# Four light experts side by side in the third and fourth expert stages of a diffusion trunk

## The chip, the cores and the metric

The kernel runs on one core of a Trainium2 chip. The metric is the device time of one execution, in microseconds (us). The engines are TensorE (PE, matrix products), VectorE (DVE), ScalarE (ACT), GpSimd (POOL) and SyncE (SP, whose queue issues the transfers from HBM); SBUF is the on-chip memory of 128 partitions, PSUM the eight banks of 128 x 512 float32 that TensorE writes.

## The reference

One inference step of a trunk of four layers over 256 tokens (128 context, 128 latent) of 1024 channels. Each layer has a token mixer (in turn Hyena convolution, gated linear attention, FNet transform, pooling) and then a mixture of experts, each with normalization and a conditioned shift and scale. The change touches the experts:

```python
def hier_moe(h, w_rg, w_re, w1, w3, w2):
    ...
    p_grp, g_idx = lax.top_k(pg, 1)                       # one of 4 groups
    ...
    pe_top, e_idx = lax.top_k(jax.nn.softmax(le, axis=-1), 2)   # two of its 4 experts
    ...
    hid = jax.nn.silu(jnp.einsum('nd,xdf->nxf', xt, w1)) * jnp.einsum('nd,xdf->nxf', xt, w3)
    y = jnp.einsum('nxf,xfd->nd', hid * combine[..., None].astype(hid.dtype), w2)
```

There are 16 experts, each with w1 and w3 of 1024 x 512 and w2 of 512 x 1024, all float32. A token uses two of the 16, so an expert sees 32 of the 256 tokens on average.

## The kernel before

**The expert stage.** Every expert is computed for 64 slots (`SLOTS`): a selection matrix `sel`, built by VectorE from the tokens' ranks within an expert (`build_sel`), gathers tokens into slots by matmul (`gather`), and a transposed one scatters the results back (`scatter`). If an expert has more than 64 tokens, a further round of all experts runs (`rounds_known`, `far_rounds`); with these inputs none is needed. Experts p and p + 8 form pair p, eight pairs per stage, p0 to p7 (`PAIRS`), computed side by side in TensorE: the stationary operand is the 128 x 64 block of gathered tokens of one expert, the moving one 512 columns of its weights, and the two experts of a pair write the two halves of the partitions of one bank, in different column groups of the array. A pair takes 8 steps of the contraction for w1 (`experts_in`, kind 0), 8 for w3 (kind 1), and 4 for each of the two halves of w2's output (`experts_out`, kind 2). Between w1, w3 and w2 TensorE does the previous pair's scatter, a part of the next couple's gather and two kinds of transposes. Two pairs form a couple (`COUPLES`), which share one `sel`.

**The weights' way in.** One list, `piece_stream()`, fixes the order in which all weights are loaded by SyncE's queue: conditioning maps (`ada`), mixer weights, experts. They go through a ring of 14 slots (`RING`) of 8 KB per partition, that is 1.049 MB or one slab each. A matrix of a pair is four slabs (`SLABS`, q = 0 to 3); slab q holds the contraction's rows 2q and 2q + 1 (of eight blocks), for both experts. For pairs after the first, two slabs go in one transfer of 2 MB (`in_halves`, `second_half`). Before each transfer SyncE waits until the slot's last content has been used, by counters that TensorE raises (`freed`, `h1_mm`, `h3_mm`, `y_mm`); its queue is strictly in order, so what stands behind a waiting transfer waits with it. Four more slabs have a home in another part of SBUF (`homes`): first the w2 of p0, loaded ahead during the mixer (`first_w2`), and after that the w1 of p2 (`homed`), as soon as p0's w2 has been used. Ahead of a stage are thus loaded: w2, w1 and w3 of p0, w1 of p1 and half of its w3.

**Routing.** After the router's matmul VectorE works out, in a chain of small instructions that each wait for the one before (`chain`), each token's group, its two experts, their shares (`comb`) and its rank in each (`rank`), then the number of rounds. In the first three stages a conditioning map is computed beside it (`beside`, `ada_rows`, `ada_mod`).

Of the kernel before, what the change touches and what calls it, by code (L numbers as in the profile page):

```python
# [19 lines left out]
G = 2  # L20
# [12 lines left out]
PAIRS = EXPERTS // 2  # L33
RING = 14
# [86 lines left out]
def piece_stream():  # L121
# [26 lines left out]
    for i in range(LAYERS):  # L148
        experts = [("moe", i, p, kind, q) for p in range(PAIRS) for kind in range(3) for q in range(SLABS)
                   if p or kind < 2]  # L150
# [20 lines left out]
def homed(what):  # L171

    return what[0] == "moe" and what[2:4] == (2, 0)


def in_halves(what):

    return what[0] == "moe" and what[2] > 0 and what[2:4] != (PAIRS - 1, 2)


def second_half(what):
    return in_halves(what) and what[4] % 2 == 1


def build(nc, a):
# [21 lines left out]
    with ctx:  # L207
# [22 lines left out]
        over = sb("over", [1, 2], I32)  # L230
        bank = [ctx.enter_context(nc.psum_tensor(f"bank{i}", [P, 512], F32)) for i in range(8)]
# [59 lines left out]
        selw = ar(7168, 2, G, 2, SLOTS)  # L291
        rt = ar(7424, 240)
        comb = ar(7680, G, EXPERTS)
        memb = ar(7712, EXPERTS).bitcast(BF16).rearrange("p (g n) -> p g n", g=G)
        rank = ar(7744, G, EXPERTS)
        wcol = ar(7816, 1)
# [4 lines left out]

        def home_pair(i, h):
            return ar(homes[i][h], 2 * SLAB)
# [53 lines left out]
        def freed(what):  # L357
# [14 lines left out]
            if k == "moe":  # L372
                return USED[what[3]], primed(SLABS * (PAIRS * what[1] + what[2]) + what[4] + 1)
# [17 lines left out]
        def expert_slab(n, q):  # L391
            return a["moe_w"][bass.ds(n, 1)][:, :, SLAB * (q % 2):SLAB * (q % 2) + SLAB].rearrange("o p n -> p (o n)")

# [41 lines left out]
        def _(sp):  # L437
# [4 lines left out]
            last = {}  # L442
            for what, slot, nth in stream:
# [8 lines left out]
                if what[0] == "first":  # L452
# [8 lines left out]
                    for q in range(SLABS):  # L461
                        sp.dma_start(first_w2[i][q], expert_slab(6 * PAIRS * i + 4 + q // 2, q)) \
                            .then_inc(s("first_w2_loaded"), 16)
# [4 lines left out]
                if what[0] == "moe" and what[1] < LAYERS - 1 and what[2:] == (1, 1, 2):  # L468
# [10 lines left out]
                    sp.dma_start(rw[:], a["router"][i + 1]).then_inc(s("rw_loaded"), 16)  # L479
                if homed(what):  # L480
                    _, i, p, kind, q = what
                    if q % 2:
                        sp.wait_ge(s("y_mm"), primed(SLABS * PAIRS * i + q + 1))
                        sp.dma_start(home_pair(i, q // 2), a["moe_w"][6 * (PAIRS * i + p) + 2 * kind + q // 2]) \
                            .then_inc(s(f"homed{q // 2}"), 16)
                    continue
# [3 lines left out]
                last[slot] = freed(what)  # L490
                if in_halves(what):
                    _, i, p, kind, q = what
                    if q % 2:
                        sp.dma_start(ring_all[:, SLAB * (slot - 1):SLAB * (slot + 1)],
                                     a["moe_w"][6 * (PAIRS * i + p) + 2 * kind + q // 2]) \
                            .then_inc(s(f"full{slot - 1}"), 16)
                    continue
                if what[0] == "moe":
                    _, i, p, kind, q = what
                    src = expert_slab(6 * (PAIRS * i + p) + 2 * kind + q // 2, q)  # L500
                else:
                    src = source(what)
                sp.dma_start(ring[slot], src).then_inc(s(f"full{slot}"), 16)

            def one_round(b, i):
                for kind in range(3):
                    sp.wait_ge(s(USED[kind]), primed(SLABS * PAIRS * (i + 1)))
                with sp.Fori(0, COUPLES) as c:
                    for j in range(2):
                        for kind in range(3):  # L510
                            sp.wait_ge(s("fb_" + USED[kind]), primed(SLABS * (2 * (b + c) + j)))
                            for q in range(SLABS):
                                sp.dma_start(ring[where["moe", i, 1, kind, q][0]][:],
                                             expert_slab(6 * (PAIRS * i + j) + 2 * kind + q // 2 + 12 * c, q)) \
                                    .then_inc(s(f"fb_full{kind}"), 16)
                for kind in range(3):
                    sp.wait_ge(s("fb_" + USED[kind]), primed(SLABS * 2 * (b + COUPLES)))
# [143 lines left out]
        def _(pe):  # L661
# [102 lines left out]
            def experts_in(pre, n, kind, x, j, weights, ready):  # L764

                for q in range(SLABS):
                    w = weights(kind, q).rearrange("p k (e n) -> p k e n", e=2)
                    ready(q)
                    for kk in range(2):
                        k = 2 * q + kk  # L770
                        for e in range(2):
                            at = P * e + SLOTS * j
                            last = mm(bank[4 + kind][SLOTS * e:SLOTS * e + SLOTS, :], x[:, k, at:at + SLOTS],  # L773
                                      w[:, kk, e, :], start=k == 0, stop=k == KD - 1)
# [8 lines left out]
            def slot_weights(pre, n, j):  # L783
                for g in range(G):
                    last = tr(bank[5][:, g * P:g * P + P], selw[:, j, g].rearrange("p e n -> p (e n)"), ident)
                last.then_inc(s(pre + "selT_mm"), 1)

            def experts_out(pre, n, weights, ready):
                pe.wait_ge(s(pre + "hidT_ready"), primed(n + 1))
                for q in range(SLABS):  # L790
                    w = weights(2, q).rearrange("p f (e n) -> p f e n", e=2)
                    if q % 2 == 0:
                        ready(q // 2)
                    for ff in range(2):
                        f = 2 * (q % 2) + ff
                        for e in range(2):
                            last = mm(bank[6 + q // 2][SLOTS * e:SLOTS * e + SLOTS, :],  # L797
# [1222 lines left out]
```

## Time and profile before

| | |
|---|---|
| median of 3 runs | 1402.37 us (1401.28 to 1403.22) |
| profiled execution, its own time | 1400.19 us |
| its span, first to last instruction | 1398.0 us |
| TensorE busy | 1343.8 us, 96% |
| VectorE busy | 473.5 us, 34% |
| moved by DMA | 554.37 MB, mean 397 GB/s |
| mean granted clock of TensorE | 0.995 |

Busy time is the time in which at least one instruction of an engine runs. The float32 matmuls appear as two records each, and records of different column groups overlap, so that the busy time of a group of rows divided by its count, not the mean of one record, is what one record costs. The chain of work that ended last goes back from the last instruction to whatever released it, step by step. The granted clock is given as a share of TensorE's full clock.

### The profile page before, as it was taken

To read this page: it belongs to the slowest core of one execution; us is meant where nothing else is said; L and a number is where in the kernel's file an instruction comes from. 1 tells how busy PE (TensorE), PEld (TensorE's weight loads), DVE (VectorE), ACT (ScalarE), POOL (GpSimd) and SP (SyncE) were. 2 spreads that over 40 slices of the span, in tenths; PEclk is the share of its full clock that TensorE was granted. 3 is DMA by queue.
4 is the path that set the end of the run, shared out by engine and by line. 5 is a ranking of instruction groups with operands and counts; after the bars stand their busy time and mean duration, and the time that the engine had idled before them with its cause. 6 is when DMAs were issued, how large, how long until landed. Compare 5 with 4: busy or idle time off the path is not lost.

```text
span 1398.0 us, 17305 instructions
## 1 busy us (share of the span) xinstructions
PE 1343.8 (96%) x7140; PEld 743.5 (53%) x7140; DVE 473.5 (34%) x1067; ACT 286.2 (20%) x514; POOL 32.1 (2%) x30
## 2 busy tenths in 40 slices
PE   9999999999988899999999988999999999999996
PEld 4786585444434688775444424854444356444433
DVE  3787514111114797624112113141111144111113
ACT  3311024111103122224111103241111035111102
POOL 0001310000000000010000000100000000000000
PEclk9999999999999999999999999999999999999999
DMA  9997999999999995789999999889999998999995
GB/s 384 420 398 271 421 420 414 428 427 427 428 428 418 422 406 227 264 357 407 428 426 428 428 428 419 349 364 414 427 428 428 427 419 359 407 426 428 427 427 210
DMA packets 55654, 554.37 MB, mean 397 GB/s; under 512 B 6097, under 2 KB 8081, under 8 KB 9233
## 3 DMA queue, kind: packets, MB, share of 16 engines
q1 hardware_dynamic: 53792, 551.19, 94.7%
q10 hardware_dynamic: 1778, 2.01, 0.4%
q8 instruction: 59, 0.97, 0.3%
q14 instruction: 25, 0.20, 0.0%
HBM read 551.08 MB, written 2.10 MB: 396 GB/s over the span
## 4 chain that ended last, share of the span: by engine, by line
PE 79%; DMA 16%; DVE 2%; ACT 1%; SPq 1%; issue 0%; POOL 0%; DVEq 0%; POOLq 0%
PE bank L773 26%; PE bank L719 14%; PE bank L797 13%; DMA ring<-in_moe_w 10%; PE bank L738 5%; DMA ring<-in_w_ada 4%; PE bank L756 4%; PE bank L679 3%; PE bank L565 2%; DMA ring<-in_hy_w_in 2%; PE bank L693 2%; PE bank L549 1%; PE bank L1022 1%; PE bank L906 1%; PE bank L629 1%; PE bank L623 1%
## 5 line engine op out<-in xcount | busy, mean ns | idle before, releaser
L773 PE MATMUL bank<-ring,hT 128*64 128x512 f32 x1024 | 225.3, 594 | 0.0
L773 PE MATMUL bank<-ring,arena 128*64 128x512 f32 x896 | 199.6, 595 | 22.3 <-DMA ring<-in_moe_w 22.3
L797 PE MATMUL bank<-ring,arena 128*64 128x512 f32 x896 | 198.5, 595 | 0.0
L1533 DVE TENSOR_TENSOR rows<-rows,bank 128x512 f32<-128x512 f32 x32 | 22.0, 688 | 456.5 <-PE bank L773 456.5
L773 PEld LDWEIGHTS bank<-ring,hT 128*64 128x64 f32 x1024 | 72.1, 137 | 139.3 <-issue 137.6
L773 PEld LDWEIGHTS bank<-ring,arena 128*64 128x64 f32 x896 | 63.8, 137 | 150.7 <-issue 128.3
L797 PEld LDWEIGHTS bank<-ring,arena 128*64 128x64 f32 x896 | 61.7, 137 | 116.9 <-issue 115.2
L1552 DVE SCALAR_TENSOR_TENSOR yv_rest<-bank,arena,yv_big 128x512 fp32r<-128x512 f32 x64 | 48.0, 750 | 199.9 <-ACT yv_big L1221 199.9
L719 PE MATMUL bank<-hT,ring 128*128 128x256 f32 x512 | 112.0, 380 | 0.3 <-DMA ring<-in_hy_w_in 0.3
L719 PEld LDWEIGHTS bank<-hT,ring 128*128 128x128 f32 x512 | 96.6, 190 | 15.1 <-issue 2.2
L1221 ACT ACTIVATE yv_big<-bank,arena 128x512 fp32r<-128x512 f32 x64 | 44.0, 688 | 281.0 <-PE bank L797 281.0
L719 PE MATMUL bank<-arena,ring 128*128 128x256 f32 x384 | 83.8, 380 | 1.6 <-DVE arena L1746 0.9
L719 PEld LDWEIGHTS bank<-arena,ring 128*128 128x128 f32 x384 | 72.6, 190 | 12.6 <-DVE arena L1746 1.2
L679 PE MATMUL bank<-ring,condT 128*32 128x512 f32 x576 | 69.1, 598 | 2.5 <-DMA ring<-in_w_ada 1.8
L738 PE MATMUL bank<-sel,htok_big 128*128 128x256 f32 x256 | 68.0, 301 | 0.8 <-DVE sel L1520 0.8
L756 PE MATMUL bank<-selT,yv_big 128*128 128x256 f32 x256 | 66.7, 297 | 1.7 <-DVE yv_rest L1552 1.7
L738 PE MATMUL bank<-sel,htok_rest 128*128 128x256 f32 x256 | 63.2, 282 | 0.0
L756 PEld LDWEIGHTS bank<-selT,yv_big 128*128 128x128 f32 x256 | 48.0, 188 | 28.5 <-issue 26.0
L756 PE MATMUL bank<-selT,yv_rest 128*128 128x256 f32 x256 | 62.2, 279 | 0.0
L1214 ACT ACTIVATE rows<-bank 128x512 f32<-128x512 f32 x32 | 19.1, 598 | 206.2 <-PE bank L773 206.2
L738 PEld LDWEIGHTS bank<-sel,htok_big 128*128 128x128 f32 x256 | 48.3, 189 | 23.7 <-issue 20.5
L1485 DVE CUSTOM_DVE_ANT_0 arena<-ring,vec 128x1024 bf16<-128x1024 f32 x48 | 58.2, 1275 | 6.3 <-DMA ring<-in_w_ada 6.2
(227 smaller groups left out, 1375.8 us busy)
## 6 DMA issues: line engine op xcount, KB each, us to landing
ring<-in_moe_w SPq DMA_DIRECT2D x152, 2048.0 KB, 18.5
ring<-in_w_ada SPq DMA_DIRECT2D x96, 1024.0 KB, 14.8
ring<-in_moe_w SPq DMA_DIRECT2D x48, 1024.0 KB, 23.6
arena<-in_moe_w SPq DMA_DIRECT2D x16, 1024.0 KB, 14.6
arena<-in_moe_w SPq DMA_DIRECT2D x8, 2048.0 KB, 9.7
ring<-in_hy_w_in SPq DMA_DIRECT2D x12, 1024.0 KB, 27.3
ring<-in_hy_w_out SPq DMA_DIRECT2D x4, 1024.0 KB, 14.0
ring<-in_gla_w_v SPq DMA_DIRECT2D x4, 1024.0 KB, 26.2
```

Source lines behind the costliest of these rows:

```text
L565: last = mm(bank[b][:, 256 * (c % 2):256 * (c % 2) + 256], hT[:, k, g], w8[:, k, :], start=k == 0, stop=k == KD - 1)
L679: last = mm(ada_bank(n)[32 * j:32 * j + 32, :], condT[:, G * k:G * k + 32], w[:, j, :], start=k == 0, stop=k == KD - 1)
L693: ins = mm(bank[6][:, 0:NT], ones[:], hT[:, k].rearrange("p g t -> p (g t)"), start=k == 0, stop=k == KD - 1)
L719: last = mm(dst, w[:, k, (m % 2) * P:(m % 2) * P + P], (hT[:, k] if rhs is None else rhs[:, k]).rearrange("p g t -> p (g t)"), start=k == ...
L738: last = mm(bank[b][:, (k % 2) * NT:(k % 2) * NT + NT], htok[n % 2][:, n // 2, k * P:k * P + P], sel[:, n // 2].rearrange("p e j n -> p (e ...
L756: last = mm(half(m), part[:, m * P:m * P + P], selT[:], start=first_pair and m % 2 == 0 and part is yv[0], stop=False, skip_group_check=True)
L773: last = mm(bank[4 + kind][SLOTS * e:SLOTS * e + SLOTS, :], x[:, k, at:at + SLOTS], w[:, kk, e, :], start=k == 0, stop=k == KD - 1)
L797: last = mm(bank[6 + q // 2][SLOTS * e:SLOTS * e + SLOTS, :], hidT[:, f, SLOTS * e:SLOTS * e + SLOTS], w[:, ff, e, :], start=f == 0, stop= ...
L1221: act_fn(yv[0][:, 512 * h:512 * h + 512], bank[6 + h][:], ACT.Identity, scale=wcol) \
L1485: v.tensor_tensor_reduce(junk[at % len(junk)], w, cond_wide[n][:, g], 1.0, b_ada(i, 16 * q + j, 1), ALU.mult, ALU.add, mod[:, i, 16 * q + ...
L1533: tt(sil[:], sil[:], bank[5][:], ALU.mult).then_inc(s(pre + "hid_ready"), 1)
L1552: stt(yv[1][:, cols], bank[6 + h][:], wcol, yv[0][:, cols].bitcast(F32), ALU.mult, ALU.subtract) \
```

## The change

In the third and fourth expert stages (`QUADS`, layers 2 and 3 counted from 0) the eight pairs become six pairs and one unit of four experts with 32 slots each. VectorE sorts the 12 experts outside pairs 0 and 1 by their number of tokens (`order_experts`); the four lightest form the last unit, and SyncE reads the order from SBUF (`value_load`) and loads each pair's weights by it. If one of the four has more than 32 tokens, a further round runs. The weights of these stages are stored expert by expert: a transfer of 2 MB brings both halves of the contraction of one expert's matrix, in the order of slabs 0, 2, 1, 3 (slab 2h + e is half h of expert e). The matrix of p2 with a home is now w2 (kind 2) instead of w1 (kind 0). TensorE's counters rise once per half of a matrix instead of once per slab, in all four stages. In the first three stages the copy `ada_rows` moves ahead of the shares.

```diff
+QUAD = PAIRS - 2
+QUAD_SLOTS = 32
+QUADS = (2, 3)
+UNITS_TO = [sum(QUAD + 1 if i in QUADS else PAIRS for i in range(n)) for n in range(5)]
...
+        if i in QUADS:
+            experts = [("moe", i, p, kind, q) for p in range(QUAD) for kind in range(3)
+                       for q in ((0, 2, 1, 3) if p else range(SLABS)) if p or kind < 2]
+            experts += [("moe", i, p, kind, 2 * h + e) for kind in range(2) for p in (QUAD, QUAD + 1) for e in range(2)
+                        for h in range(2)]
+            experts += [("moe", i, p, 2, 2 * h + e) for h in range(2) for p in (QUAD, QUAD + 1) for e in range(2)]
...
 def homed(what):
-    return what[0] == "moe" and what[2:4] == (2, 0)
+    return what[0] == "moe" and what[2:4] == (2, 2 if what[1] in QUADS else 0)
...
 def second_half(what):
-    return in_halves(what) and what[4] % 2 == 1
+    return in_halves(what) and (what[4] >= 2 if what[1] in QUADS else what[4] % 2 == 1)
...
-                return USED[what[3]], primed(SLABS * (PAIRS * what[1] + what[2]) + what[4] + 1)
+                return USED[what[3]], primed(2 * (UNITS_TO[what[1]] + (min(what[2], QUAD) if what[1] in QUADS else what[2])) + what[4] // 2 + 1)
...
+                if what[0] == "moe" and what[1] in QUADS and what[2] >= FIXED and what[3:] == (0, 0):
+                    i, p = what[1:3]
+                    sp.wait_ge(s("order_known"), QUADS.index(i) + 1)
+                    for e in range(2):
+                        n = (PAIRS - FIXED) * e + p - FIXED
+                        expert[p, e] = sp.value_load(order[0:1, n:n + 1], min_val=EXPERTS * QUADS.index(i),
+                                                      max_val=EXPERTS * QUADS.index(i) + EXPERTS - 1)
...
+            def columns(j, quad=False):
+
+                if quad:
+                    return [(P * e + SLOTS * jj, QUAD_SLOTS) for jj in range(2) for e in range(2)]
+                return [(P * e + SLOTS * j, SLOTS) for e in range(2)]
+
+            def experts_in(pre, i, n, kind, x, cols, weights, ready):
+
+                for h in range(2):
+                    ws = weights(kind, h)
+                    for kk in range(4):
+                        k = 4 * h + kk
+                        if kk % 2 == 0:
+                            ready(k // 2)
+                        for o, (at, m) in enumerate(cols):
+                            last = mm(bank[4 + kind][m * o:m * o + m, :], x[:, k, at:at + m], ws[o][kk] if i not in QUADS else ws[o][:, kk, :],
+                                      start=k == 0, stop=k == KD - 1)
                     last.then_inc(s(pre + USED[kind]), 1)
...
+            def order_experts(i):
+
+                N, each = ORDERED, [P, ORDERED, 2, PAIRS - FIXED]
+                chain(v.tensor_copy(two(o_key12), later(o_key)))
+                chain(tt(o_cmp, o_key12.unsqueeze(1).broadcast_to([P, N, N]), o_key12.unsqueeze(2).broadcast_to([P, N, N]),
+                         ALU.is_ge))
+                chain(v.reduce_sum(o_pos, o_cmp, AX.X))
...
+                ordered(two(o_id), iota[:, 0:EXPERTS])
+                ts(order[0:1, :], o_id[0:1, :], EXPERTS * QUADS.index(i) - 1.0, None, ALU.add).then_inc(s("order_known"), 1)
+                for values, out in ((rank, rank0), (comb, comb0)):
+                    for g in range(G):
+                        ordered(later(out[:, g]), values[:, g])
...
-                build_sel("", 0)
+                build_sel("", 0, rank)
+                if beside is not None:
+                    ada_rows(beside)
                 dve.wait_ge(s("route_exp"), 2 * i + 1)
...
+                if i in QUADS:
+                    order_experts(i)
...
-                if beside is not None:
-                    ada_rows(beside)
                 moe_round(i, beside)
```

## Rows read from the trace of the kernel before

**Rows 1.** The page: busy time, GB/s in 40 slices, chain's shares by engine.

```profile
PE 1343.8 (96%) x7140; PEld 743.5 (53%) x7140; DVE 473.5 (34%) x1067; ACT 286.2 (20%) x514; POOL 32.1 (2%) x30
...
GB/s 384 420 398 271 421 420 414 428 427 427 428 428 418 422 406 227 264 357 407 428 426 428 428 428 419 349 364 414 427 428 428 427 419 359 407 426 428 427 427 210
...
PE 79%; DMA 16%; DVE 2%; ACT 1%; SPq 1%; issue 0%; POOL 0%; DVEq 0%; POOLq 0%
```

**Rows 2.** Windows of the third and fourth expert stages; last columns: clock, DMA share, GB/s.

```profile
952.00:956.00 4.00, 4.00 (x22) 1.37 (x20) 0.75 (x1) 0.69 (x1) 0.00 (x0) 1.00 0.85 283
976.00:1100.00 124.00, 124.00 (x642) 52.97 (x639) 19.92 (x32) 14.65 (x23) 0.00 (x0) 1.00 1.01 427
1198.00:1202.00 4.00, 4.00 (x22) 1.42 (x20) 0.75 (x1) 0.69 (x1) 0.00 (x0) 1.00 0.69 217
1202.00:1340.00 138.00, 138.00 (x716) 59.30 (x714) 22.11 (x36) 17.14 (x27) 0.00 (x0) 1.00 1.01 428
```

**Rows 3.** Chain that ended last: start us, us, what (L773 w1 and w3, L797 w2).

```profile
932.31 13.88 PE bank L773 x64
...
955.97 6.87 PE bank L773 x32
...
964.91 7.02 PE bank L773 x32
...
981.71 6.87 PE bank L773 x32
...
1129.86 7.04 PE bank L797 x32
...
1376.00 7.04 PE bank L797 x32
```

**Rows 4.** Timeline of TensorE, p7's w3 in the third stage; in brackets its idle time before.

```profile
1118.65 3.65 PE L773 MATMUL bank<-ring,arena 128*64 128x512 f32 x16 [1.33 <-DMA ring<-in_moe_w]
1123.46 3.65 PE L773 MATMUL bank<-ring,arena 128*64 128x512 f32 x16 [1.15 <-DMA ring<-in_moe_w]
```

**Rows 5.** The page's costliest groups: busy us, mean ns of one, idle before.

```profile
L773 PE MATMUL bank<-ring,hT 128*64 128x512 f32 x1024 | 225.3, 594 | 0.0
...
L679 PE MATMUL bank<-ring,condT 128*32 128x512 f32 x576 | 69.1, 598 | 2.5 <-DMA ring<-in_w_ada 1.8
```

**Rows 6.** Timeline of SyncE's queue at five issues: start us, us, line.

```profile
942.85 0.33 SPq L494 DMA_DIRECT2D ring<-in_moe_w  x1
...
952.57 0.33 SPq L484 DMA_DIRECT2D arena<-in_moe_w  x1
...
962.92 0.33 SPq L494 DMA_DIRECT2D ring<-in_moe_w  x1
...
1199.08 0.33 SPq L484 DMA_DIRECT2D arena<-in_moe_w  x1
...
1209.43 0.33 SPq L494 DMA_DIRECT2D ring<-in_moe_w  x1
```

**Rows 7.** The page's DMA issues: count, KB each, median us from issue to landing.

```profile
arena<-in_moe_w SPq DMA_DIRECT2D x8, 2048.0 KB, 9.7
```

**Rows 8.** Timeline of VectorE, end of the third stage's routing and first product after.

```profile
928.97 0.19 DVE L1645 TENSOR_TENSOR arena<-arena 128x32 f32<-128x32 f32 x1
929.20 0.53 DVE L1648 TENSOR_SCALAR arena<-arena 128x1 f32<-128x1 f32 x3
...
932.74 0.18 DVE L1468 SCALAR_TENSOR_TENSOR scale<-mod,vec 128x16 f32<-128x16 f32 x1
946.35 0.69 DVE L1533 TENSOR_TENSOR rows<-rows,bank 128x512 f32<-128x512 f32 x1 [13.43 <-PE bank L773]
```

**Rows 9.** Windows about the second mixer's start: us, PE busy, PEld, DVE, ACT, POOL, clock.

```profile
470.00:475.00 5.00, 1.82 (x8) 1.26 (x8) 1.94 (x3) 3.08 (x6) 0.00 (x0) 0.98 1.02 423
475.00:480.00 5.00, 3.78 (x11) 3.24 (x12) 3.72 (x8) 1.75 (x2) 0.00 (x0) 0.50 1.03 426
480.00:485.00 5.00, 5.00 (x21) 4.23 (x21) 4.78 (x9) 0.00 (x0) 0.00 (x0) 0.84 1.00 413
```

More of the change, by code:

```diff
@@ L389, in build, with pair_matrix, expert_matrix, slab @@
         USED = ["h1_mm", "h3_mm", "y_mm"]
-        def expert_slab(n, q):
-            return a["moe_w"][bass.ds(n, 1)][:, :, SLAB * (q % 2):SLAB * (q % 2) + SLAB].rearrange("o p n -> p (o n)")
+        def pair_matrix(i, kind, h, p):
+            n = 6 * (PAIRS * (i - sum(m < i for m in QUADS)) + p) + 2 * kind + h
+            return a["moe_w"][bass.ds(n, 1)]
+        def expert_matrix(kind, n):
+            return a["moe_q"][bass.ds(len(QUADS) * EXPERTS * kind + n, 1)]
+        def slab(i, kind, q, p, expert=None):
+            if i in QUADS:
+                n = EXPERTS * QUADS.index(i) + PAIRS * (q % 2) + p if expert is None else expert
+                m, at = expert_matrix(kind, n), q // 2
+            else:
+                m, at = pair_matrix(i, kind, q // 2, p), q % 2
+            return m[:, :, SLAB * at:SLAB * at + SLAB].rearrange("o p n -> p (o n)")
+        def halves(i, kind, x):
+            if i in QUADS:
+                return [[x(2 * h + e).rearrange("p (k n) -> p k n", k=4) for e in range(2)] for h in range(2)]
+            return [[[x(2 * h + kk // 2).rearrange("p (k e n) -> p k e n", k=2, e=2)[:, kk % 2, e] for kk in range(4)]
+                     for e in range(2)] for h in range(2)]
         def prime(eng, *names):
@@ L441, in _ @@
             sp.dma_start(vec[:], a["vec"]).then_inc(s("vec_loaded"), 16)
-            last = {}
+            last, expert = {}, {}
             for what, slot, nth in stream:
@@ L490, in _ @@
                 last[slot] = freed(what)
+                if what[0] == "moe":
+                    _, i, p, kind, q = what
+                    chosen = expert[p, q % 2] if i in QUADS and p >= FIXED else None
                 if in_halves(what):
[L492 to L495, printed above, removed]
+                    if second_half(what):
+                        if i in QUADS:
+                            n = EXPERTS * QUADS.index(i) + PAIRS * (q % 2) + p if chosen is None else chosen
+                            both = expert_matrix(kind, n)
+                        else:
+                            both = pair_matrix(i, kind, q // 2, p)
+                        sp.dma_start(ring_all[:, SLAB * (slot - 1):SLAB * (slot + 1)], both.rearrange("o p n -> p (o n)")) \
                             .then_inc(s(f"full{slot - 1}"), 16)
@@ L498, in _ @@
                 if what[0] == "moe":
-                    _, i, p, kind, q = what
-                    src = expert_slab(6 * (PAIRS * i + p) + 2 * kind + q // 2, q)
+                    src = slab(i, kind, q, p, chosen)
                 else:
```

198 lines of the change are left out of this document (118 added, 80 removed).

## The prediction

> **What bounds the kernel now.** I read the page first: TensorE is busy 96% of the span and the chain of work that ended last is 79% TensorE and 16% DMA [rows 1]. That invites the thought that each TensorE microsecond removed is a microsecond won. The GB/s line speaks against it: the slices of the expert stages stand at 418 to 428, and 428 looks like a ceiling. So I cut the last two expert stages into windows [rows 2]. From 976 to 1100 us and from 1202 to 1340 us the queue moves 427 and 428 GB/s without a break, and the only idle DMA time inside the two stages is where a stage begins.
>
> The two rates, from rows: a pair of experts takes 25.74 us of TensorE (981.71 less 955.97, [rows 3]), and 12 slabs of 1.049 MB, which at 428 GB/s take 2.45 us each, 29.4 us. TensorE is the faster. It lives off what was loaded ahead (14 ring slabs and 4 home slabs, 44 us of transfer) and has used that up by the last pairs: in pair 7 it stops for 1.33 and 1.15 us before two slabs each, and the starts lie 4.8 us apart [rows 4], which is the transfer time of two slabs. So the stage ends when the last slab lands. The matrix h3 of pair 7 is complete at 1123.46, four slabs are still to come, the last at 1123.46 + 9.8 = 1133.3, and the output matmuls end at 1129.86 + 7.04 = 1136.90, 3.6 us behind it [rows 3, 4]. The fourth expert stage repeats this some 246 us later (1376.00 for 1129.86).
>
> The length of such a stage is thus: when the queue starts again after the prefetch is used up, plus the slabs left at 2.45 us each, plus 3.6 us. TensorE's own work is not in that sum.
>
> **What the change takes away.** A unit of 25.74 us in each of two stages. Four experts of 32 columns need as many steps as two of 64: a pair's step is four matmul records of 220 ns (225.3 us over 1024), 0.88 us; a four-expert step would be eight. The conditioning maps already run four 32-column groups side by side: 69.1 us over 576 records is 120 ns, 0.96 us for eight [rows 5]. The eight units become seven, and the last has 24 steps dearer by at most 0.08 us. TensorE is relieved of 25.7 - 1.9 = 23.8 us per stage, 48 in all. By the sum above this is waiting time moved, not time won: worth 0. The Trainium skill (TensorEngine Tiling (Array Packing), When to Use Tiling) promises up to 4x for at most 32 columns, twice what 64 columns get; the trace agrees to within a tenth. If the stages were bound by TensorE, that would give 1402.4 - 47.6 = 1354.8; DMA windows without a gap exclude it.
>
> The bytes stay the same: each expert's matrices are still loaded once.
>
> **What the change moves: the ring.** Two things change in the stream of the two stages. A 2 MB transfer now brings one expert's whole matrix, first and second half of the contraction, where before it brought half of the contraction for both experts. Both its slots are free only when the *whole* previous matrix pair there has been used. And pair 2's matrix at home is now w2, not w1. I walked the queue for the third stage, with p0, p1 for the pairs, and slots counted from the stage's first slab. Before the walk both kernels are alike: p0's w1 and w3 lie in slots 0 to 7, p1's w1 in 8 to 11, half its w3 in 12 and 13, and the rest of p1 is issued up to 942.85 us into slots 0 to 5 [rows 6].
>
> Before: the next in order are pair 2's w1 slabs, at home, free as soon as p0's w2 is used: issued at 952.57 (and 956). DMA idled a little around it: 952 to 956 has 283 GB/s, which is 4 x (1 - 283/428) = 1.4 us lost [rows 2, 6].
>
> After: p2's w1, first expert, goes to slots 6 and 7, which p0's w3 leaves at 932.31 + 13.88 = 946.2 [rows 3]. That is one transfer, 4.9 us of work for the queue. The next, p2's w1 of the second expert, goes to slots 8 and 9, which now hold the *whole* of p1's first expert's w1, used until 955.97 + 6.87 = 962.8; the trace has an issue at 962.92 that waited for just this event [rows 6]. Everything behind it in SyncE's order waits too, pair 2's w2 as well, though its home is long free. So the queue restarts 962.8 - 952.6 = 10.3 us later and has 4.9 us more to do meanwhile: a loss of 5.4 us, a gap of 1.4 + 5.4 = 6.8 us.
>
> Behind the gap I followed each transfer at 4.9 us against the end of the matrix whose slots it takes. A 2 MB transfer that finds the queue nearly empty lands 9.7 us after its issue [rows 7]; those of 962.9 land at 972.6 and 977.5, and the third is due at 982.4. Its slots come free at 964.91 + 7.02 = 971.9, so that it can land at 981.6: the tightest place, 0.8 us in hand. None later idles the queue, and TensorE, in pairs 2 to 5, waits at most 1.5 us. So the gap is never made up, and the last slab lands 5.4 us late, at 1138.7.
>
> **The four-expert unit.** It needs eight slabs before its first matmul (before: two), its w3 eight more, its w2 four and four. By counting back from 1138.7: w1 complete at 1099.4, w3 at 1119.0, w2's first half at 1128.9. TensorE ends pair 5 near 1087, so it idles some 12 us, works 7.4 (1106.8), idles 12, works 7.4 (1126.4), does scatter and transposes in 2.7 us as now, and has the last half of w2's four steps, 3.6 us, left when the last slab lands: 1142.3 against 1136.9, again +5.4. The ring holds 14 slabs and w1 keeps eight: w3's last transfer waits for w1's end at 1106.8, can land 9.7 later at 1116.5, and is due at 1119.0. A margin of 2.5 us.
>
> **The stage after.** The queue and TensorE both enter the fourth mixer 5.4 us late, so the short stall of the queue at that stage's start stays as it is. In the fourth stage the same walk gives 1209.43 - 1199.08 = 10.35 [rows 6], less 4.9 again: +5.4, on a gap of 4 x (1 - 217/428) = 2.0 us [rows 2].
>
> **What is hidden.** The ordering adds some 24 VectorE instructions per stage. Chained small ones cost 0.2 us each here (928.97 is followed by the next at 929.20), those of 144 elements lie between that and the 0.69 us of 512; I take 0.3, 7 us in all, bounds 5 and 16. They cover themselves: VectorE is through at 932.9 and idle 13.4 us until 946.35 [rows 8]. TensorE asks for the new selection at 946.2; at 16 us it would be late by about 3 us, at 7 not at all. The ids that SyncE waits for are ready after the first seven, near 932, long before 943; two register loads follow. The time between 942.85 and 946.2 covers them, and data are then queued until 953. The earlier copy of the conditioning rows moves 0.7 us within the same slack. In the first two stages counts per half instead of per slab can make the last half wait up to 0.5 us for its second slab: +0.3 taken.
>
> **The sum.** 1398.0 of span becomes 1398.0 + 5.4 + 5.4 + 0.3 = 1409.1; the profiled execution took 1400.19, and the median of the runs, 1402.37, lies 2.2 above that. On the median: **1413.5 us**.
>
> **Rivals.**
>
> *The clock.* Between 470 and 480 us TensorE idled 4.4 us, and the granted clock went to 0.50, the lower level, 1.2 GHz [rows 9]; 12 us of idling twice per stage will do so too. If it stays low through the eight steps of w1, they take 14.7 and end at 1114.1; w3's last transfer lands at 1123.8, 4.8 late, and the stage ends that much later. In this trace the low level lasted 5 us and then 0.16/0.5 x 5 = 1.6 more, which costs 3.3 of work: w1 ends at 1110.1, the transfer is 0.8 late, and I leave that to the range. The Trainium skill (TensorE: Matmul & The Clock Gate, HAM oscillation) describes this very pattern, short compute between DMA waits, as one that loses the clock each time; here it would be 1413.5 + 2 x 5 = 1423. For it: the idles are nearly three times the one seen. Against: the loss seen would be hidden but for 0.8. Chance 0.14.
>
> *No gap.* If the queue has other work after 958, or the transfers left are taken faster, both effects vanish and the time is 1402.7. Speaking for it: only my walk through slots, no row, shows the gap; a slot miscounted by two would close it. Chance 0.13.
>
> *Faster.* One mechanism: the transfer issued at 946.2 fills the gaps that the queue has now (1.4 and 2.0 us), and nothing opens in their place; it decides if pair 2's second transfer is issued before 956. Then 1402.4 - 3.4 = 1399.0. A larger gain needs the queue above 428 GB/s, which no window shows. Chance 0.07.
>
> *The light experts are not light enough.* With over 32 tokens for one of the four, a whole further round runs: at least 96 slabs x 2.45 = 235 us, 1640. Counted from the reference's inputs, the four lightest of the twelve have 17, 19, 29, 31 and 19, 22, 26, 30 tokens against 32 slots: held, but 31 by a single token. Chance 0.03.
>
> **Chances and range.** My forecast has 0.63, its own range 1409 to 1418. A measurement of this kernel tells 0.2%, 2.8 us, from no change. Slower: 0.63 + 0.14 + 0.03 = 0.80; within: 0.13; faster: 0.07. The range 1402 to 1422 takes in the forecast, the case of no gap and the smaller half of the clock's.
>
> **What would show it.** About 7 us of idle DMA some 25 us into the third and fourth expert stages, between a transfer issued at the end of p0's w3 and one at the end of p1's w1; TensorE idling 10 us or more before each matrix of the four-expert unit; a granted clock of 0.5 there; DMA at 427 to 428 between; TensorE busy some 45 us less and the span longer. It is wrong if the four-expert unit begins without a DMA wait, or if the queue never idles behind pair 0.

## The result and the profile after

The changed kernel takes 1418.01 us in the median of 4 runs, the kernel before on the same chips 1401.82: ratio 1.0118, 95% interval 1.0100 to 1.0136, 16.2 us slower, and the interval leaves out 1. The forecast was 1413.5, 11.1 us slower; the sign and most of the size are as forecast. The profiled execution has a span of 1414.8 us, 16.8 more than before.

The page of the changed kernel, first its busy time, GB/s and the chain by engine:

```profile
PE 1310.4 (93%) x7096; PEld 729.3 (52%) x7096; DVE 476.8 (34%) x1099; ACT 282.1 (20%) x508; POOL 32.1 (2%) x30
...
GB/s 384 421 385 271 420 421 417 425 428 427 427 426 420 421 414 207 284 346 427 424 428 426 429 422 389 328 427 343 427 426 428 422 421 339 335 428 428 427 425 178
...
PE 77%; DMA 19%; DVE 2%; ACT 1%; issue 1%; POOL 0%; SPq 0%; DVEq 0%; POOLq 0%
```

TensorE is busy 33.4 us less than in [rows 1] and the kernel is longer. (Some 45 us less were forecast; the low clock in the four-expert unit, seen below, gives back about 12: its long rows add up to 47.6 us, and would be 35.6 at the 7.07 and 3.64 us that they take at full clock.) Two new hollows stand in the GB/s line, 343 and 335, each a slice behind the start of an expert stage. SyncE's queue at the issues behind pair 0 of the third stage:

```profile
946.12 0.35 SPq L542 DMA_DIRECT2D ring<-in_moe_q  x1
...
962.74 0.34 SPq L542 DMA_DIRECT2D ring<-in_moe_q  x1
...
971.85 0.33 SPq L542 DMA_DIRECT2D ring<-in_moe_q  x1
```

These are the three times that the prediction worked out by its walk through the ring, 946.2, 962.8 and 971.9. Where [rows 6] have an issue at 952.57, nothing is issued now for 16.6 us. Windows (us, PE busy, PEld, DVE, ACT, POOL, granted clock, DMA share, GB/s): two about this gap, three in the third stage's four-expert unit, one at the start of the fourth stage, two about the gap's twin there, and one at the last matmuls of that stage:

```profile
952.00:958.00 6.00, 6.00 (x30) 2.01 (x28) 1.50 (x2) 1.38 (x2) 0.00 (x0) 1.00 0.94 401
958.00:966.00 8.00, 8.00 (x46) 3.86 (x44) 0.00 (x0) 0.60 (x1) 0.00 (x0) 1.00 0.35 92
1092.00:1105.00 13.00, 4.97 (x24) 1.38 (x28) 0.00 (x0) 0.00 (x0) 0.00 (x0) 0.50 1.00 427
1112.00:1122.00 10.00, 2.48 (x12) 0.68 (x16) 0.00 (x0) 0.00 (x0) 0.00 (x0) 0.52 1.00 419
1139.00:1143.00 4.00, 3.61 (x20) 1.27 (x24) 0.00 (x0) 0.00 (x0) 0.00 (x0) 0.58 1.00 418
1184.00:1193.00 9.00, 9.00 (x53) 4.71 (x53) 7.09 (x27) 3.55 (x5) 0.00 (x0) 1.00 0.29 80
1205.00:1218.00 13.00, 13.00 (x65) 4.73 (x62) 1.50 (x2) 1.97 (x3) 0.00 (x0) 1.00 0.52 220
1218.00:1222.00 4.00, 4.00 (x26) 2.15 (x26) 0.00 (x0) 0.00 (x0) 0.00 (x0) 1.00 0.93 311
1394.00:1400.00 6.00, 5.92 (x32) 1.52 (x32) 0.00 (x0) 0.00 (x0) 0.00 (x0) 0.58 0.01 3
```

Idle DMA in the gap of the third stage: 6 x (1 - 401/428) + 8 x (1 - 92/428) = 6.7 us (forecast 6.8); in the fourth: 13 x (1 - 220/428) + 4 x (1 - 311/428) = 7.4 us (forecast 7.4). The four-expert unit is in the timeline of TensorE, for the third and the fourth stage:

```profile
1100.03 9.76 PE L825 MATMUL bank<-ring,arena 128*32 128x512 f32 x64 [12.47 <-DMA ring<-in_moe_q]
1119.53 8.55 PE L825 MATMUL bank<-ring,arena 128*32 128x512 f32 x64 [9.73 <-DMA ring<-in_moe_q]
...
1130.72 3.64 PE L849 MATMUL bank<-ring,arena 128*32 128x512 f32 x32
1139.39 5.34 PE L849 MATMUL bank<-ring,arena 128*32 128x512 f32 x32 [5.04 <-DMA ring<-in_moe_q]
...
1354.75 8.70 PE L825 MATMUL bank<-ring,arena 128*32 128x512 f32 x64 [12.49 <-DMA ring<-in_moe_q]
1374.24 9.19 PE L825 MATMUL bank<-ring,arena 128*32 128x512 f32 x64 [10.79 <-DMA ring<-in_moe_q]
1386.11 3.64 PE L849 MATMUL bank<-ring,arena 128*32 128x512 f32 x32
1394.08 6.08 PE L849 MATMUL bank<-ring,arena 128*32 128x512 f32 x32 [4.33 <-DMA ring<-in_moe_q]
```

w1, w3 and the last half of w2 wait for their last slab, as forecast, at 1100.0, 1119.5 and 1139.4 (forecast 1099.4, 1119.0, 1138.7); the first half of w2, at 1130.72, does not wait. New is the length of the last row of either stage: the same 32 records take 3.64 us at 1130.72 and 5.34 and 6.08 us at the end, where the windows show a mean granted clock of 0.58. The third stage ends at 1144.8, the fourth at 1400.2, where [rows 3] give 1136.9 and 1383.0: 7.9 and 17.2 us late.

VectorE's part is where it was put: it is through with routing, ordering and selection at 937.9, and then idles 8.2 us, where [rows 8] had 13.4.

```profile
937.68 0.17 DVE L1528 SCALAR_TENSOR_TENSOR scale<-mod,vec 128x16 f32<-128x16 f32 x1
946.02 0.69 DVE L1603 TENSOR_TENSOR rows<-rows,bank 128x512 f32<-128x512 f32 x1 [8.16 <-PE bank L825]
```

### The profile page after: what moved, and what is told of

Its sections match the earlier page's. It is cut to its first block, busy times and chain, and to the rows that moved or that the text cites. A ratio compares the mean times of both kernels' runs of the same rounds, so it can differ in the third digit from the quotient of the medians.

```text
span 1414.8 us, 17531 instructions
## 1 busy us (share of the span) xinstructions
PE 1310.4 (93%) x7096; PEld 729.3 (52%) x7096; DVE 476.8 (34%) x1099; ACT 282.1 (20%) x508; POOL 32.1 (2%) x30
## 4 chain that ended last, share of the span: by engine, by line
PE 77%; DMA 19%; DVE 2%; ACT 1%; issue 1%; POOL 0%; SPq 0%; DVEq 0%; POOLq 0%
PE bank L825 25%; PE bank L765 14%; PE bank L849 11%; DMA ring<-in_moe_q 9%; DMA ring<-in_moe_w 8%; PE bank L784 4%; PE bank L725 3%; PE bank L802 3%; DMA ring<-in_w_ada 2%; PE bank L611 2%; PE bank L739 2%; PE bank L595 1%; PE bank L1082 1%; PE bank L966 1%; PE bank L675 1%; PE bank L669 1%
## 5 line engine op out<-in xcount | busy, mean ns | idle before, releaser
L825 PE MATMUL bank<-ring,arena 128*64 128x512 f32 (+1 forms) x960 | 194.3, 634 | 57.8 <-DMA ring<-in_moe_q 45.5
L849 PE MATMUL bank<-ring,arena 128*64 128x512 f32 (+1 forms) x832 | 175.3, 617 | 10.2 <-DMA ring<-in_moe_q 9.4
L825 PEld LDWEIGHTS bank<-ring,arena 128*64 128x64 f32 (+1 forms) x960 | 61.7, 136 | 183.0 <-issue 168.9
L849 PEld LDWEIGHTS bank<-ring,arena 128*64 128x64 f32 (+1 forms) x832 | 54.8, 136 | 113.5 <-issue 112.0
L1622 DVE SCALAR_TENSOR_TENSOR yv_rest<-bank,arena,yv_big 128x512 fp32r<-128x512 f32 x60 | 45.0, 751 | 202.7 <-ACT yv_big L1281 202.7
L802 PE MATMUL bank<-selT,yv_big 128*128 128x256 f32 x240 | 62.2, 296 | 1.8 <-DVE yv_rest L1622 1.8
L802 PEld LDWEIGHTS bank<-selT,yv_big 128*128 128x128 f32 x240 | 45.0, 188 | 27.1 <-issue 24.4
L802 PE MATMUL bank<-selT,yv_rest 128*128 128x256 f32 x240 | 58.1, 279 | 0.0
## 6 DMA issues: line engine op xcount, KB each, us to landing
ring<-in_w_ada SPq DMA_DIRECT2D x96, 1024.0 KB, 14.7
```

Of the source, the lines that this page charges most:

```text
L802: last = mm(half(m), part[:, m * P:m * P + P], selT[:], start=first_pair and m % 2 == 0 and part is yv[0], stop=False, skip_group_check=True)
L825: last = mm(bank[4 + kind][m * o:m * o + m, :], x[:, k, at:at + m], ws[o][kk] if i not in QUADS else ws[o][:, kk, :], start=k == 0, stop=k ...
L849: last = mm(bank[6 + h][m * o:m * o + m, :], hidT[:, f, m * o:m * o + m], ws[o][f] if i not in QUADS else ws[o][:, f, :], start=f == 0, st ...
L1622: stt(yv[1][:, cols], bank[6 + h][:], wcol, yv[0][:, cols].bitcast(F32), ALU.mult, ALU.subtract) \
```

## The experiments

All ratios are to the kernel before, run on the same chip. Because the profiled executions reach the third stage up to 4.6 us apart, the last columns give each stage by itself in that execution, from its first expert matmul to its last, and the landing of its last slab, read as the start of the matmul that it released; both come from the chain or TensorE's timeline. A dash: TensorE did not wait for that slab, so the time is not seen. "Filling" matmuls (`keep_running`) are products on ones into an unused bank, put where TensorE would idle.

| kernel | ratio (95%) | third stage | fourth stage | last landing, 3rd / 4th |
|---|---|---|---|---|
| before | 1 | 204.6 | 204.2 | - |
| changed | 1.0118 (1.0100 to 1.0136) | 212.8 | 213.5 | 207.4 / 207.4 |
| e1, w1 at home | 1.0071 (1.0050 to 1.0091) | 210.1 | 210.4 | 204.7 / 204.8 |
| e2, clock kept | 1.0103 (1.0076 to 1.0130) | 212.8 | 213.3 | 207.5 / 206.9 |
| e3, both | 1.0072 (1.0052 to 1.0093) | 209.4 | 210.1 | 204.0 / 203.6 |
| e4, no unit | 1.0142 (1.0116 to 1.0168) | 214.0 | 215.5 | - |
| e5, before, TensorE lighter | 0.9976 (0.9968 to 0.9985) | 204.5 | 202.8 | 202.5 / 200.8 |
| e6, single slabs | 1.0086 (1.0073 to 1.0099) | 209.3 | 210.5 | 203.4 / 204.4 |
| e7, e6 and clock | 1.0057 (1.0044 to 1.0070) | 207.9 | 208.3 | 204.2 / 204.6 |
| e8, e7 and end split | 1.0033 (1.0021 to 1.0045) | 207.3 | 206.8 | - / 204.8 |
| e9, clock at the end only | 1.0094 (1.0078 to 1.0109) | 210.8 | 210.9 | 207.2 / 207.2 |
| e10, e9 and end split | 1.0093 (1.0077 to 1.0109) | 210.5 | 210.9 | - |
| e11, mixed | 1.0026 (1.0015 to 1.0036) | 206.8 | 205.1 | - / 203.1 |
| e12, before, single slabs | 1.0026 (1.0017 to 1.0034) | 205.6 | 205.3 | 203.7 / - |

The mixer between the two stages is 41.9 us in every one of them.

**Does TensorE's work count? e5.** In the kernel before:

```diff
-                            last = mm(bank[4 + kind][SLOTS * e:SLOTS * e + SLOTS, :], x[:, k, at:at + SLOTS],
-                                      w[:, kk, e, :], start=k == 0, stop=k == KD - 1)
+                            wide = P if pre == "" and kind == 1 and q > 1 and n >= 2 * PAIRS and n % PAIRS > 1 else 512
+                            last = mm(bank[4 + kind][SLOTS * e:SLOTS * e + SLOTS, 0:wide], x[:, k, at:at + SLOTS],
+                                      w[:, kk, e, 0:wide], start=k == 0, stop=k == KD - 1)
```

> The kernel before, with less work for TensorE in the third and fourth stages and nothing else changed: in pairs 2 to 7 the second half of w3's contraction is computed for 128 of its 512 columns, so a part of the result is left out. It relieves TensorE of 2.6 us per pair, 16 per stage, 32 in all, and loads the same bytes in the same order. Theory (the stages end with the last slab): within 2 us of the kernel before. Rival (TensorE bounds them): 1402 - 32 = 1370.

Measured 1399.12 against 1402.26, 3.1 us less. The 32 us were reckoned too high: by the page TensorE's busy time fell by 23.6 us, from 1343.8 to 1320.2. The last rows of TensorE's w2 in the third and in the fourth stage:

```profile
1135.70 1.94 PE L798 MATMUL bank<-ring,arena 128*64 128x512 f32 x8 [0.55 <-DMA ring<-in_moe_w]
...
1380.37 1.94 PE L798 MATMUL bank<-ring,arena 128*64 128x512 f32 x8 [0.53 <-DMA ring<-in_moe_w]
```

TensorE now waits for the very last slab and does two steps behind it. In the fourth stage that slab lands 200.8 us after the start; in the kernel before TensorE ended at 204.2, 3.4 behind (I had inferred 3.6 from counting slabs). In the third it is 202.5, so that there I had 3.6 where 2.1 is right. This takes e5's landings for those of the kernel before, whose own trace does not show them. Relief thus buys a part of TensorE's lag behind the last landing, not its work: 0.1 and 1.4 us by the two stages of the table, 3.1 by the medians, for 23.6 us less of work. The difference between the two readings was not traced.

**The gap, and the clock. e1, e2, e3.** e1 puts home w1 back, e2 fills the unit's idle time, e3 does both:

```diff
-    return what[0] == "moe" and what[2:4] == (2, 2 if what[1] in QUADS else 0)
+    return what[0] == "moe" and what[2:4] == (2, 0)
```
```diff
+                    if quad:
+                        pe.wait_ge(s("yv_rest"), primed(2 * n))
+                        keep_running(11, wide_ones)
                     experts_in("", i, n, 0, x, cols, weights, gathered_for)
+                    if quad:
+                        keep_running(12, wide_ones)
...
-                    experts_out("", i, n, cols, weights, evacuated)
+                    experts_out("", i, n, cols, weights, (lambda h: keep_running(3 * h, wide_ones)) if quad else evacuated)
```

> The changed kernel with one thing put back: in the third and fourth expert stages the matrix of pair 2 that has a home is w1 again, not w2. Transfers stay one expert's whole matrix each. Theory (the queue's gap behind pair 0): w1's four slabs are issued at about 952 and 956 us, so the gap at 958 to 965 us closes (about 1.4 us of idle DMA left, as before the change), and so does that of the fourth stage; the queue ends each stage 5.4 us earlier than in the changed kernel: 1418.0 - 10.8 = 1407, or a little less. Rival (the four-expert unit with its slow clock costs it all, the gap being made up later): no change, 1416 to 1418.

> The changed kernel with idle-time matmuls on ones into an unused bank in the four-expert unit: 11 before w1, 12 before w3, 3 before the second half of w2, so that TensorE never idles there for long. Theory: the granted clock stays at 1.00, w1 and w3 take 7.2 us instead of 9.8 and 8.6, w2's last half 3.6 instead of 5.3 and 6.1; the stages end 2.5 us (third) and about 6 us less late (fourth, with the start of the stage), so 1418.0 - 6 = 1412, near the sum in which the clock was left out (1413.5). The gap of the queue behind pair 0 stays at 6.7 and 7.4 us. Rival (the clock is a bystander, the transfers land late by themselves): within 2 us of 1418.

> Both of the former in one: pair 2's w1 at home and the idle-time matmuls. Theory: both losses are gone and the saved unit is worth nothing, since the last slab lands when it did before: 1401 to 1403, the time of the kernel before within 0.2%. Rival (TensorE's relief of some 24 us per stage is worth something once nothing else is in its way): under 1398.

e1 won 2.7 and 3.1 us in the two stages, against 5.4 expected in each. The rest is seen in its windows of the third stage:

```profile
952.00:962.00 10.00, 10.00 (x49) 3.30 (x46) 1.50 (x2) 1.38 (x2) 0.00 (x0) 1.00 0.90 331
1000.00:1015.00 15.00, 15.00 (x80) 6.27 (x80) 3.04 (x6) 2.57 (x4) 0.00 (x0) 1.00 0.97 386
```

The big gap has shrunk to 10 x (1 - 331/428) = 2.3 us, but the queue now runs short again at 1000 to 1015, by 1.5 us, which my walk had not looked for: with the queue no longer late, transfers that need a whole matrix's slots find them not yet free. (In the same window e11, whose pairs 1 to 3 go slab by slab, has 422 GB/s, and the kernel before 430.) So the home is about half of the loss and the whole-matrix transfers keep the other half.

e2's ratio, 1.0103, cannot be told from the 1.0118 of the changed kernel, and its stages are 0.0 and 0.2 us shorter, though w1 and w3 now took 7.1 us each. The slow clock in w1 and w3 is harmless to within that, as the prediction's margin had it. The last half of w2 still took 5.34 and 6.40 us: three filling matmuls end 3.5 us before the landing, and behind that pause the clock is low again. e3 therefore keeps that loss too, and came out at 1412, not at 1402. My theory for these three was wrong in its sums, and three terms were open: the end, the whole-matrix transfers, and the steps behind the last landing.

**The clock at the end. e9.**

```diff
                 for h in range(2):
+                    if len(cols) == 4:
+                        keep_running((0, 5)[h], wide_ones)
                     ws = weights(2, h)
```

> The changed kernel with five idle-time matmuls before the last half of the unit's w2 and none elsewhere. Theory (of the slow clock only the last half of w2 costs anything, since w1 and w3 have slack in front of the next landing): that half takes 3.6 us instead of 5.4 and 6.1, 1418 - 4.2 = 1413.8, though w1 and w3 still run at the lower clock. Rival (the clock costs through w1 and w3, which release the slots late): 1417 to 1419.

Measured 1414.26, 1.0094 against 1.0118. TensorE's timeline, w1, w3 and the last half of w2 in the third stage, and the last half in the fourth:

```profile
1099.76 9.85 PE L825 MATMUL bank<-ring,arena 128*32 128x512 f32 x64 [12.51 <-DMA ring<-in_moe_q]
1119.23 8.66 PE L825 MATMUL bank<-ring,arena 128*32 128x512 f32 x64 [9.62 <-DMA ring<-in_moe_q]
...
1139.10 3.64 PE L851 MATMUL bank<-ring,arena 128*32 128x512 f32 x32 [0.38 <-DMA ring<-in_moe_q]
...
1391.92 3.64 PE L851 MATMUL bank<-ring,arena 128*32 128x512 f32 x32 [0.49 <-DMA ring<-in_moe_q]
```

w1 and w3 are as slow as in the changed kernel; the last half is back to 3.64, 1.7 and 2.4 us shorter, and the stages are 2.0 and 2.6 us shorter. The intervals of the two ratios just overlap; the rows carry this, not the medians. With e2 this separates the two places at which the clock falls.

**The stream without the unit. e4.** Eight pairs in every stage, ordering and transfers kept:

```diff
-QUAD = PAIRS - 2
+QUAD = PAIRS
...
-UNITS_TO = [sum(QUAD + 1 if i in QUADS else PAIRS for i in range(n)) for n in range(5)]
+UNITS_TO = [PAIRS * n for n in range(5)]
```

> The changed kernel without the four-expert unit: eight pairs in all stages, the ordering of the twelve experts, its instructions and register loads kept, transfers of one expert's whole matrix, pair 2's w2 at home. Theory: the stream alone costs 5.4 us per stage, 1401.8 + 10.8 = 1412.6, with gaps of 6.8 and 7.4 us behind pair 0 and the clock at 1.00. Rival (the unit is the cost): the time of the kernel before, 1402.

1423.09, a ratio of 1.0142, where 1412.6 was expected. It has the gap (154 GB/s from 958 to 966 us) and a second loss which I had left out. A pair's w3 can now begin only when all four of its slabs are there; pair 7's w3 and last w2 in the third stage, then its w3 in the fourth:

```profile
1131.03 7.09 PE L822 MATMUL bank<-ring,arena 128*64 128x512 f32 x32 [1.01 <-DMA ring<-in_moe_q]
...
1140.79 7.09 PE L846 MATMUL bank<-ring,arena 128*64 128x512 f32 x32
...
1386.84 8.78 PE L822 MATMUL bank<-ring,arena 128*64 128x512 f32 x32 [3.12 <-DMA ring<-in_moe_q]
```

so that 7.1 + 2.7 + 7.1 us of work follow w3's landing, against 3.65 + 2.7 + 7.1 before. The clock was not full either, as expected it was: in the fourth stage w3 took 8.78 us instead of 7.09, at a mean granted clock of 0.81, behind a pause of 3.12 us, and that lies on the path to the end. The four-expert unit escapes the longer tail, because it waits long for w2 anyway. The unit, then, is not the cost. Within this stream it wins 3.2 us by the two stages together and 3.4 by the ratios, whose intervals overlap.

**Single slabs. e6, e7, e12.** e6 has w1 at home and the stream below in the two stages; e7 adds filling matmuls before the halves of the unit's matrices; e12 is the kernel before with single slabs in all four stages and nothing else. First from e6, then e12:

```diff
+                       for q in range(SLABS) if p or kind < 2]
+            experts += [("moe", i, p, kind, 2 * h + e) for kind in range(3) for h in range(2) for p in (QUAD, QUAD + 1)
+                        for e in range(2)]
...
-    return what[0] == "moe" and what[2] > 0 and not last
+    return what[0] == "moe" and what[1] not in QUADS and what[2] > 0 and not last
```
```diff
-    return what[0] == "moe" and what[2] > 0 and what[2:4] != (PAIRS - 1, 2)
+    return False
```

> The changed kernel with w1 of pair 2 at home and with its stream in slabs of 1 MB in the two stages: first the first half of the contraction of all experts of a unit, then the second, each slab waiting for its own slot only. The storage by expert, the ordering and the four-expert unit stay. Theory (transfers of whole matrices hold slots too long, and with home w1 that still cost 2.5 to 3 us of idle DMA per stage): idle DMA in the third stage as before the change (under 2.5 us, against 4.9 and 7.8), the last slab lands 201 us after the stage's first expert matmul, as before, and what is left is the slow clock at the end of the last unit, 1.7 to 2.7 us per stage: 1403 to 1407. Rival (1 MB transfers, or register addresses, are slower to move): 1412 as with the home alone.

> The former with idle-time matmuls in the four-expert unit, before each half of a matrix (0, 3, 6, 6, 3, 6 of them), six before the last half of w2. Theory: the granted clock stays 1.00 through the last half, which takes 3.6 us and not 5.4 or 6.4: 1401 to 1403, the time before. Rival (the clock at the end is not what is left): as the former.

> The kernel before, all four stages in pairs, with one thing changed: the experts' slabs in the ring go in transfers of 1 MB, each waiting for its own slot, and not two at a time. Theory (the kernels with 1 MB slabs in the third and fourth stages moved 421 GB/s in mid-stage where those with 2 MB move 427, and that is the size's doing, not that of the storage or of the ordered experts): 421 GB/s in mid-stage here too, 1.4% of some 185 us or 2.7 us per stage, with two to four stages that bind: 1407 to 1412. Rival (the finer release of slots wins, the rate is due to something else in the changed kernel): 1402 or less, 427 GB/s.

e6 has hardly a gap left where the changed kernel had its own, here in the third and in the fourth stage:

```profile
952.00:956.00 4.00, 4.00 (x22) 1.31 (x20) 0.64 (x1) 0.69 (x1) 0.00 (x0) 1.00 1.00 379
956.00:960.00 4.00, 4.00 (x22) 1.42 (x20) 0.87 (x2) 0.69 (x1) 0.00 (x0) 1.00 0.96 377
...
1203.00:1207.00 4.00, 4.00 (x22) 1.39 (x20) 0.37 (x1) 0.69 (x1) 0.00 (x0) 1.00 0.76 289
1207.00:1215.00 8.00, 8.00 (x40) 2.62 (x38) 1.13 (x2) 0.69 (x1) 0.00 (x0) 1.00 0.97 387
```

That is 0.9 and 2.1 us against 428 GB/s, where the kernel before has 1.4 and 2.0. But e6 took 1414.21, in part for a reason that I had only as the rival: the rate. (The other part is the clock at the end, 5.9 and 6.1 us for the last half.) Windows of 60 us in mid-stage, first of e6, then of e12, then of the changed kernel in its fourth stage:

```profile
1010.00:1070.00 60.00, 59.93 (x316) 26.38 (x312) 9.31 (x15) 7.02 (x12) 0.00 (x0) 1.00 1.01 421
```
```profile
1010.00:1070.00 60.00, 60.00 (x311) 25.69 (x308) 9.32 (x15) 7.63 (x12) 0.00 (x0) 1.00 1.01 421
```
```profile
1240.00:1300.00 60.00, 60.00 (x316) 26.43 (x314) 8.57 (x14) 6.94 (x11) 0.00 (x0) 1.00 1.01 429
```

e12 shows it in the kernel before: the same bytes in transfers of 1 MB (8 KB per partition) move at 421 GB/s and not at 427 to 428 (the kernel before in the same windows), and the kernel is 0.26% slower. Over 185 us the rate is 2.7 us per stage; e12's stages are only 1.0 and 1.1 us longer. Finer release may give the rest back; no run shows that by itself. e7 won 4 us over e6: its last halves take 3.64 us each. Still, its stages are 3.3 and 4.1 us longer than before.

**Steps behind the last landing. e8, e10.** The last four slabs in two parts, all first parts ahead of all second ones. TensorE waits for the first parts ahead of its first step and for the second ones ahead of its third (those lines are left out here):

```diff
+                if what[0] == "moe" and i in QUADS and p >= QUAD and kind == 2 and q > 1:
+                    sp.dma_start(ring[slot][:, 0:1024], src[:, 0:1024]).then_inc(s("tail"), 16)
+                    tails.append((slot, src))
+                    if len(tails) == 4:
+                        for slot, src in tails:
+                            sp.dma_start(ring[slot][:, 1024:2048], src[:, 1024:2048]).then_inc(s(f"full{slot}"), 16)
```

> The former with the last four slabs of the unit's w2 loaded in two parts of 0.5 MB each, first the first two blocks of the contraction of all four experts, then the last two, so that two steps and not four are left when the last byte lands. Theory (a stage is the landing of its last slab plus what TensorE still has to do behind it): 1.8 us less per stage than the former, 1398 to 1400, a little under the kernel before; this is the one thing that TensorE's relief can buy. Rival (transfers of 0.5 MB cost as much more): no better than the former.

> The former with the last four slabs of w2 in two parts of 0.5 MB each, as before, so that two steps and not four follow the last landing. Theory: 1.7 us less per stage than the former, 1410.4; what is then left over the kernel before is the queue's gap behind pair 0, twice some 5.8 us, less the 1.4 that TensorE no longer adds at the end. Rival (the number of steps behind the landing is not a term): 1413.8.

In e8's fourth stage the last landing releases two steps instead of four:

```profile
1387.69 1.93 PE L867 MATMUL bank<-ring,arena 128*32 128x512 f32 x16
1390.01 1.92 PE L867 MATMUL bank<-ring,arena 128*32 128x512 f32 x16 [0.40 <-DMA ring<-in_moe_q]
```

The landing is 204.8 us after the start, as in e7 (204.6), and the stage ends 1.5 us earlier; the medians differ by 2.7. In e8's third stage TensorE does not wait for the slabs at all: six filling matmuls (5.4 us) run up to the last half. In e10 nothing was won. There, in both stages, five filling matmuls (4.6 us) still ran when the first parts had landed, so that TensorE, not the queue, set the end: a filling matmul that is too late costs its own time. e10 is thus no evidence on the steps.

**All of it. e11.**

```diff
+WHOLE = 4
...
+                       for q in ((0, 2, 1, 3) if p >= WHOLE else range(SLABS)) if p or kind < 2]
```

> All of it: pair 2's w1 at home, slabs of 1 MB for pairs 1 to 3, where slots are scarce, whole matrices of 2 MB from pair 4 on, where they are not, idle-time matmuls in the unit, w2's last slabs in two parts. Theory: the queue has no gap beyond that of the kernel before and moves 427 GB/s from pair 4 on (421 in the kernels with 1 MB throughout), so that the last slab lands as in the kernel before or 0.7 us later, and two steps follow: 1400 to 1404, even with the kernel before. Rival (the relief of TensorE is worth something of its own once all this is gone): under 1398.

1406.19, the best variant of the changed kernel, and still 0.26% above the kernel before, outside the 1400 to 1404 expected. Its rate in mid-stage is 427 again. Its fourth stage takes 205.1 us, 0.9 more than before; its last slab lands at 203.1, 2.3 us later than in e5, for which no run gives the cause. Its third takes 206.8, 2.2 more; there, as in e10, the last half began only when the filling ended:

```profile
1126.92 3.64 PE L867 MATMUL bank<-ring,arena 128*32 128x512 f32 x32
1130.49 5.44 PE L980 MATMUL bank<-ones 128*128 128x512 f32 x12
1135.86 1.49 PE L867 MATMUL bank<-ring,arena 128*32 128x512 f32 x12
```

No variant that computes the whole result beat the kernel before.

## Why the prediction came out as it did

**TensorE's relief is worth nothing: right.** 33 us of busy time went, and the time rose. e5 settles it in the kernel before but for a small part: 3.1 us for 23.6.

**The walk through the ring: right, to a tenth or so.** Three issue times and two gaps (6.7 and 7.4 us) are as worked out. Less the old 1.4 and 2.0 they account for 5.3 + 5.4 = 10.7 us of the 17.2 by which the last expert matmul is late. I gave the coarse release and the home as one cause with one price. e1 shows that they are two: taking the home alone back returns only half, since the next whole-matrix transfers then find their slots taken. The stall of the queue at the fourth stage's start did not stay as it was: it grew from 5.7 us (1176 to 1186 us in the kernel before, at 184 GB/s) to 7.3 (1184 to 1193, at 80), since TensorE comes later than the queue. It cost nothing more: counted from the stage's start the last slab lands at 207.4 in both stages.

**The queue at the unit: right.** w3's last transfer was issued at 1110.04, as worked out for the low clock (1110.1), and no gap opened; e2 shows that a full clock there gains at most 0.5 us at the landing.

**The unit's end: the term mis-sized.** I wrote that the last half of w2 has "four steps, 3.6 us, left when the last slab lands". It took 5.34 and 6.08 us. I had looked for the low clock only where TensorE idles 12 us, in w1, and not at the idle of 4 to 5 us before the very last half, the only one with no slack behind it. That is 1.7 + 2.4 = 4.1 us, shown by the rows and given back by e9. The Trainium skill (TensorE: Matmul & The Clock Gate, HAM oscillation), cited for that rival, describes short compute between DMA waits; the windows agree, 0.50 to 0.58 about the rows behind each of the unit's three waits, but its price fell at one of the three only.

**What is left.** 17.2 - 10.7 - 4.1 = 2.4 us. Most of it is a second fault in the same term. The prediction let TensorE end 3.6 us behind the last landing in the kernel before too, so that the term fell out of the difference. By e5's landings that lag was 2.1 us in the third stage and 3.4 in the fourth, while the unit's four steps take 3.6 even at the full clock: 1.5 + 0.2 = 1.7 us. The rest is the landing itself: 207.4 us after the start in both stages, against e5's 202.5 and 200.8, is 11.5 us later, where the gaps make 10.7. With w3 at full clock (e2) the fourth stage's last slab landed 0.5 us sooner; the few tenths beyond that were not traced. The 0.3 us for the coarser counters in the first two stages cannot be read: the changed kernel reached the third stage 0.3 us sooner in its profiled execution, and such executions differ by more.

**The ordering, the register loads, SyncE's wait: right,** all hidden. They were not taken out by themselves, but TensorE waits for the selection 0.2 us per stage in both kernels, and VectorE has 8.2 us in hand.

**The rivals.** The clock was half right: the drop came in w1, where that rival had it, but ended sooner (9.76 us and not 14.7) and cost nothing there; its price fell at the end and was smaller (4 us, not 10). No gap, faster, and a further round are excluded by the rows.

## What to carry to other kernels

Where loads set the end of a stage, count three things before a compute saving: when the queue can restart behind the prefetch, whether any slot is now held longer, and what work follows the last landing; a saving in compute that changes none of them was worth next to nothing here. A larger transfer unit was faster per byte here but needs more slots free at once, and after a tight restart the second can outweigh the first. A wait of a few microseconds just before the last matmuls cost twice here, once as the wait and once by the clock; filling it helps only if the filling ends before the data land.

## What the runs showed of the hardware

- Transfers of 1 MB (8 KB per partition) moved 421 GB/s in mid-stage, those of 2 MB (16 KB per partition) 427 to 428, in the same kernel and place (e12 against the kernel before).
- Four column groups of 32 side by side ran within 4% of two of 64: 32 records, half of w2 for four experts, take 3.64 us at full clock, and half of w2 for a pair 3.52 (half of its 7.04 for 32 records).
- The granted clock was low behind pauses of TensorE of 2.6 to 5 us: 0.50 and 0.52 in the 3 us behind pauses of 2.60 and 2.72 us (e4, full clock before both), a mean of 0.58 behind those of 5.04 and 4.33 us (the changed kernel). Matmuls on ones ahead of a pause of 3.5 us did not keep it up (e3, where 5.34 and 6.40 us remained). It stayed at full behind pauses of 0.38 and 0.49 us (e9).
